# Modulations as rows on TensorE, the forget layer's head lengths inside its last projection block, and a delta layer without scaled keys and queries

## The chip, the cores and the metric

The kernel runs on one core of one Trainium2 chip. The metric is device time in microseconds of one execution; lower is better. All data is float32. A matmul that counts for accuracy is run as three matmuls in the type fp32r: both operands are split in a part `hi`, rounded to fp32r, and the rest `lo`, and hi·hi, lo·hi and hi·lo are added in PSUM (`triple`). Plain float32 matmuls appear in the trace as two instructions each.

## The reference

Eight layers run one after the other on x of 512 tokens by 1024. The first four are mixers (gated linear attention, spatial gating, forgetting attention, gated linear attention), each with its own modulation; the last four are dilated attention, a feed-forward layer, a gated delta layer and a feed-forward layer. What the change touches:

```
cond = silu(c)                                   # 1024 numbers
# layers 0 to 3: modulation i
mod = cond @ w_mod[i] + b_mod[i]                 # 3 x 1024: shift, scale, gate
h = rms_norm(x, norm_pre_g[i]) * (1.0 + scale) + shift
x = x + gate * rms_norm(mixer(h), norm_post_g[i])

# fox: 16 heads of 64
q, k, v, z, f_logit = split(h @ w_in)
q = rms_norm(q, g_q)                             # each head and token
k = rms_norm(k, g_k)
F = cumsum(log_sigmoid(f_logit + b_f))
o = softmax(causal(q @ k.T / 8 + F_i - F_j)) @ v
out = (o * silu(z)) @ w_out

# delta layer ("dn"): 6 heads of 128, memory of 256 tokens
qkv, z, gate_in, q_mem = split(h @ w_in)
q, k, v = split(silu(conv5(qkv)))                # 5 taps along the tokens
q = q * rsqrt(sum(q*q) + eps) * 128**-0.5
k = k * rsqrt(sum(k*k) + eps)
g = -exp(a_log) * softplus(gate_in + dt_bias);  beta = sigmoid(gate_in)
o = delta_rule(q, k, v, g, beta, chunks of 64)   # both directions, added
o = o * rsqrt(mean(o*o) + eps) * out_norm * silu(z)
mem = softmax(q_mem @ k_mem / 8) @ v_mem         # k_mem, v_mem from rms_norm(mem) @ w_kv
out = concat(o, mem) @ w_out
```

## The kernel before

The activations lie transposed in SBUF (`hT_hi`, `hT_lo`: 128 features by 8 tiles by 512 tokens). A projection is a list of blocks; a block has four chunks of 512 KB of weights (`w_raw`, six slots). For each chunk a DMA on SP's queue brings `w_raw`, ScalarE rounds it to `w_hi` (`act_feed`, L203), VectorE takes the rest to `w_lo` (`dve_feed`, L210), and TensorE runs its forms, most of them 128x512 outputs over two tiles of features, three matmuls each (L218 to L220). A block fills one of two sets of four PSUM banks, which ScalarE evacuates (`ps_evac`). Both feeds run ahead of TensorE by a few blocks, in an order written out by hand; every engine works in the order of its own program and waits on semaphores.

**Modulations.** For the first layer the 1024x2048 part of `w_mod` for shift and scale lies in four pieces in SBUF (`start_mod`, `hT_a`, `hT_b`), two tiles of rows (k) each. VectorE multiplies and adds k = 0 to 6 into `macc` (`dve_mod_first`, L490); TensorE then takes k = 7 (L500) and the sum of `macc` over the partitions (L504), both as matmuls with one column, 16 each, so that the result stands as columns. VectorE makes `modc` of it (L543, L544), and ScalarE applies it to the transposed, normed x (L752). L387 (`pe_bands`) makes tables that a later layer needs. For the layers after it the products are accumulated in `macc` by VectorE during the layer (`dve_mod`, L517, weights loaded by POOL's queue), and in the transition to the next layer `pe_mod` sums them over the partitions, again as 16 one-column matmuls (L532), and for the gate as two matmuls with 512 columns (L535). It is called `mid` there: it stands after the second chunk of the output projection, for token tiles 2 and 3; the same chunks' passes for tiles 0 and 1 come behind it and behind `g_ready`.

**The fox layer.** Blocks are projected in the order 4, 0, 1, 2, 3, 5, 6, 7 (v, q, k, v, z). After block 7, TensorE projects the 16 forget logits (`small_project`), ScalarE and VectorE make F (L1614 to L1616, L1657 to L1664), and then `norm_heads` runs for 16 tiles of 128 by 512 of q and k: ScalarE squares each (L1458), TensorE sums the squares over the heads into 32 rows of PSUM (L1445, `fox_sums`), ScalarE takes the root (L1460), VectorE the reciprocal (L1465) and its two parts (L1466, L1467), TensorE spreads a tile's rows to 128 partitions with two matmuls (L1451, L1452), and VectorE multiplies (L1470). Then the attention units begin (L1558 logits, L1560 decay, L1694 row maxima on VectorE).

**The dn layer.** Blocks 5, 0 to 4, 6 (z; q, k, v; q_mem), each of the middle ones followed by the convolution on VectorE (L2668, five taps, four tiles) and the silu on ScalarE (L2502). After block 6: 24 gate rows by `small_project`, turned (L2435), gate arithmetic (L2515 to L2519), the norm of the memory and its 16 transposes (L569 to L592, L601), the block `kv`, cumulated gates (L2446, L2447), the memory attention (L1744, L1751, L1760), and then `norm_heads` for 12 tiles with 12 rows (L1445). Only then do the six heads start: `decay_pe` (L2346), products, the inverse of a triangular matrix in doubling steps (L2323 to L2336), and the walk through the chunks with which the heads before are finished.

## Time and profile before

| | us |
|---|---|
| median of 3 runs | 2821.45 (2817.26 to 2822.45) |
| the profiled execution, device time | 2830.14 |
| its span | 2828.4 |
| TensorE busy / VectorE / ScalarE / GpSimd, of the span | 91% / 50% / 38% / 10% |

The profiled execution took 8.7 us longer than the median. The span runs from the first to the last instruction that the profiler saw. TensorE is busy in most of the 40 slices of the page; its granted clock is at full speed in most of them and at half in stretches in which it did little before. The chain that ended last tells, at each time, which engine the end waits for.

### The profile page before, as it was taken

Reading aid. Unit: us, or ns where it says so; the run is one execution under the profiler, and the core shown is the slowest. Engines: PE = TensorE matmul, PEld = TensorE weight load, DVE = VectorE, ACT = ScalarE, POOL = GpSimd, SP = SyncE. Lnnn points to the kernel's source line nnn. Section 1 sums busy time; section 2 is a strip of 40 time slices with the busy share of each in tenths; the row PEclk is TensorE's granted clock in tenths of the full one; section 3 lists DMA queues with packets and bytes.
Section 4 is the critical chain, followed back from the end, with each engine's and each line's share of the span. In section 5 each row is a group of like instructions: output and inputs, shape, how many; then the busy total and the mean of one; then the engine's idle time right before and its main releaser. Section 6 shows DMA issues by size and latency. Waiting matters only on the chain.

```text
span 2828.4 us, 32984 instructions
## 1 busy us (share of the span) xinstructions
PE 2582.8 (91%) x13022; PEld 2091.2 (74%) x13022; DVE 1410.2 (50%) x2386; ACT 1068.7 (38%) x1931; POOL 269.1 (10%) x420
## 2 busy tenths in 40 slices
PE   6989899999898989999878999999977998999998
PEld 4667778778446767787647888888854888888887
DVE  4666576555275656562244433325844666434322
ACT  4355342332443545453433322224244553322212
POOL 5233011011000013100000000001001110000000
PEclk7989999999989999999978999999977999999999
DMA  5522365256101412132101333324220000233332
GB/s 215 184 70 68 104 217 171 91 171 187 67 31 45 141 48 60 54 122 60 45 30 60 97 97 97 97 84 119 83 75 1 1 1 1 75 104 97 97 97 75
DMA packets 146228, 250.16 MB, mean 88 GB/s; under 512 B 15455, under 2 KB 65914, under 8 KB 145049
## 3 DMA queue, kind: packets, MB, share of 16 engines
q1 hardware_dynamic: 129008, 198.08, 22.4%
q0 software_dynamic: 14816, 48.31, 5.1%
q8 instruction: 104, 1.70, 0.2%
q10 hardware_dynamic: 2249, 1.65, 0.2%
q14 instruction: 51, 0.42, 0.1%
HBM read 245.84 MB, written 5.30 MB: 89 GB/s over the span
## 4 chain that ended last, share of the span: by engine, by line
PE 76%; DVE 9%; ACT 8%; DMA 3%; issue 2%; POOL 0%; SPq 0%; DVEq 0%; ACTq 0%
PE PS L218 20%; PE PS L219 19%; PE PS L220 19%; PE PS L985 2%; ACT tmp L752 1%; DMA hT_b<-in_w_mod 1%; PE PS L1760 1%; PE PS L1445 1%; DVE x L808 1%; PE PS L2323 1%; PE PS L2331 1%; PE PS L2336 1%; PE PS L1744 1%; PE PS L1581 1%; ACT w_hi L203 1%
## 5 line engine op out<-in xcount | busy, mean ns | idle before, releaser
L210 DVE TENSOR_TENSOR w_lo<-w_raw,w_hi 128x1024 fp32r<-128x1024 f32 (+1 forms) x344 | 412.7, 1207 | 782.3 <-ACT w_hi L203 781.3
L203 ACT ACTIVATE w_hi<-w_raw 128x1024 fp32r<-128x1024 f32 (+1 forms) x344 | 356.5, 1045 | 1041.9 <-DMA w_raw<-in_ffn_w_gate_up 310.1
L218 PE MATMUL PS<-hT_hi,w_hi 128*128 128x512 f32 (+1 forms) x1728 | 662.2, 383 | 21.7 <-DVE hT_lo L820 13.8
L219 PE MATMUL PS<-hT_lo,w_hi 128*128 128x512 f32 (+1 forms) x1728 | 653.3, 378 | 0.0
L220 PE MATMUL PS<-hT_hi,w_lo 128*128 128x512 f32 (+1 forms) x1728 | 653.1, 378 | 0.0
L218 PEld LDWEIGHTS PS<-hT_hi,w_hi 128*128 128x128 f32 x1728 | 331.2, 192 | 85.2 <-issue 19.0
L220 PEld LDWEIGHTS PS<-hT_hi,w_lo 128*128 128x128 f32 x1728 | 331.2, 192 | 59.9
L219 PEld LDWEIGHTS PS<-hT_lo,w_hi 128*128 128x128 f32 x1728 | 331.9, 192 | 56.6 <-issue 0.2
L218 PE MATMUL PS<-w_hi,hT_hi 128*128 128x512 f32 (+1 forms) x704 | 290.2, 412 | 32.0 <-DVE w_lo L210 7.7
L219 PE MATMUL PS<-w_lo,hT_hi 128*128 128x512 f32 (+1 forms) x704 | 278.8, 396 | 0.0
L220 PE MATMUL PS<-w_hi,hT_lo 128*128 128x512 f32 (+1 forms) x704 | 278.8, 396 | 0.0
L218 PEld LDWEIGHTS PS<-w_hi,hT_hi 128*128 128x128 f32 x704 | 141.2, 201 | 67.3 <-issue 15.1
L219 PEld LDWEIGHTS PS<-w_lo,hT_hi 128*128 128x128 f32 x704 | 141.5, 201 | 27.0 <-issue 1.8
L220 PEld LDWEIGHTS PS<-w_hi,hT_lo 128*128 128x128 f32 x704 | 140.2, 199 | 27.9
L517 DVE SCALAR_TENSOR_TENSOR macc<-mraw,cond,macc 128x512 f32<-128x512 f32 x160 | 122.1, 763 | 36.6 <-DMA mraw<-in_w_mod 33.8
L218 PE MATMUL PS<-w_hi,ffn_hi 128*128 128x512 f32 x352 | 139.4, 396 | 0.0
L220 PE MATMUL PS<-w_hi,ffn_lo 128*128 128x512 f32 x352 | 139.2, 395 | 0.0
L219 PE MATMUL PS<-w_lo,ffn_hi 128*128 128x512 f32 x352 | 139.2, 395 | 0.0
L462 POOL DMA_DIRECT2D mraw<-in_w_mod x160 | 86.3, 540 | 423.3 <-DVE macc L517 420.4
L985 PE MATMUL PS<-gla_E 128*128 128x128 f32 x448 | 62.5, 284 | 22.2 <-DVE gla_E L1204 22.1
L985 PEld LDWEIGHTS PS<-gla_E 128*128 128x128 f32 x448 | 58.2, 196 | 32.7 <-issue 30.3
L220 PEld LDWEIGHTS PS<-w_hi,ffn_lo 128*128 128x128 f32 x352 | 66.2, 188 | 16.0
(563 smaller groups left out, 3419.9 us busy)
## 6 DMA issues: line engine op xcount, KB each, us to landing
w_raw<-in_ffn_w_gate_up SPq DMA_DIRECT2D x176, 256.0 KB, 3.1
mraw<-in_w_mod POOLq DMA_DIRECT2D x160, 256.0 KB, 4.0
w_raw<-in_gla_w_in SPq DMA_DIRECT2D x48, 512.0 KB, 4.6
w_raw<-in_ffn_w_down SPq DMA_DIRECT2D x44, 512.0 KB, 3.8
w_raw<-in_fox_w_in SPq DMA_DIRECT2D x32, 512.0 KB, 4.1
w_raw<-in_sgu_w_in SPq DMA_DIRECT2D x24, 512.0 KB, 4.8
w_raw<-in_dn_w_in SPq DMA_DIRECT2D x24, 512.0 KB, 3.5
w_raw<-in_gla_w_out SPq DMA_DIRECT2D x16, 512.0 KB, 4.6
```

Of the source, the lines that this page charges most:

```text
L203: nc.scalar.activation(w_hi[:, n % NS, :, 0:m], w_raw[:, n % NS, :, 0:m], ACT.Copy).then_inc(w_hidone, 1)
L210: nc.vector.tensor_tensor(w_lo[:, n % NS, :, 0:m], w_raw[:, n % NS, :, 0:m], w_hi[:, n % NS, :, 0:m].bitcast(F32), ALU.subtract).then_inc( ...
L218: nc.tensor.matmul(o, l_hi, r_hi, start=start, stop=False)
L219: nc.tensor.matmul(o, l_hi, r_lo, start=False, stop=False)
L220: return nc.tensor.matmul(o, l_lo, r_hi, start=False, stop=stop)
L462: eng.dma_start(mraw[:, n % MS, 0, :], w[:, i % KT, m * BW:(m + 1) * BW]).then_inc(p_landed[n % MS], 16)
L517: nc.vector.scalar_tensor_tensor(out=acc, in0=mraw[:, n % MS, 0, :], scalar=cond[:, i % KT:i % KT + 1], in1=acc, op0=ALU.mult, op1=ALU.add ...
L752: ins = a.activation(tmp[:, k * P:(k + 1) * P], PS[:, 2 * t + k // 4, (k % 4) * P:(k % 4 + 1) * P], ACT.Identity, scale=nxt.scale[:, k:k + 1],
L808: v.tensor_tensor(x[:, t, :], x[:, t, :], y, ALU.add).then_inc(x_done, 1)
L985: mm = pe_.matmul(PS[:, l % 2, ts], a, m, start=True, stop=True)
L1445: t_.matmul(PS[0:nr, bank, :], sums[:, nr - per * n:2 * nr - per * n], sq(n), start=n == 0, stop=n == n_tiles - 1).then_inc(lens.sum, 1)
L1581: mm = t_.matmul(PS[rows, 5 + (h // 2) % 2, t * P:(t + 1) * P], r.v[:, k, h * FD:(h + 1) * FD], PT[:, u2 % 2, k * P:(k + 1) * P], start=k ...
```

## The change

Three parts in one kernel.

**Modulations as rows.** For the first layer, TensorE does all of it: the bias by four matmuls with one row, and for each k four matmuls with 32 columns (of `cond`, repeated 32 times) and 512 elements, which write to four groups of 32 partitions of one bank (L485, L492 in the new numbering). `dve_mod_first` and the memset ahead of it are gone; the band tables are made between k = 3 and 4. VectorE copies the bank to SBUF, TensorE turns it by four transposes (`pe_mod_turn`, L499), and VectorE makes `modc` of the columns. For layers 1 to 3 the 16 one-column matmuls become four with 32 columns, and copy, turn and `modc` follow in the same way; TensorE waits for `modc_done` ahead of the passes for tiles 0 and 1.

**Fox.** The squares of tiles 0 to 7 are made on ScalarE after the evacuation of block 5, those of 8 to 15 after that of block 6. The sums go to four column groups of one bank (tile n to rows 32·(n mod 4)), tiles 0 to 7 and the forget logits between the first and the second chunk of the last block, tiles 8 to 15 behind the second. Root, reciprocal and the two parts are made on 128 rows. The spreads of tiles 0 to 3 (`lengths`) stand between the forms of the last chunk, the other twelve behind it; the multiplication is as before. VectorE feeds the last four chunks of weights ahead of the attention behind its 16 multiplications, where it did so ahead of F before.

**Dn.** The norm of the memory moves into the first two blocks. The 12 squares are made on ScalarE behind the silu of block 2, the gate rows and the 12 sums stand ahead of block 6, the turns of the gates in the middle of it, and the turns of the lengths in the middle of `kv`. q and k are not scaled: beta is divided by |k|²+eps, the values are scaled by the root of |k|²+eps on their way out of PSUM (four ScalarE instructions in place of one), and the length of q goes into the epsilon of the output's norm (one more VectorE instruction of 128x4 a head). `norm_heads` is removed.

```diff
-        M0 = KT - 1
-
-        def dve_mod_first():
-
-            v = nc.vector
-            v.wait_ge(m_row, mod_rows(0))
-            v.wait_ge(cond_done, 1)
-            for k in range(M0):
-                if k % 2 == 0:
-                    v.wait_ge(m0_landed[k // 2], 16)
-                v.scalar_tensor_tensor(out=macc[:, 0:4 * BW], in0=first_mod[k // 2][:, k % 2, :], scalar=cond[:, k:k + 1],
-                                       in1=macc[:, 0:4 * BW], op0=ALU.mult, op1=ALU.add).then_inc(m0_used, 1)
-                v.wait_ge(m0_used, k + 1)
-
         def pe_mod_first(bank):
 
             t_ = nc.tensor
             t_.wait_ge(cond_done, 1)
-            t_.wait_ge(m0_landed[M0 // 2], 16)
-            for j in range(2 * KT):
-                t_.matmul(PS[:, bank, 2 * j:2 * j + 1], first_mod[M0 // 2][:, M0 % 2, j * P:(j + 1) * P], cond[:, M0:M0 + 1],
-                          start=j == 0, stop=False)
-            t_.wait_ge(m0_used, M0)
-            for j in range(2 * KT):
-                mm = t_.matmul(PS[:, bank, 2 * j:2 * j + 1], macc[:, j * P:(j + 1) * P], ones[:, 0:1],
-                               start=False, stop=j == 2 * KT - 1)
+            t_.wait_ge(m_row, mod_rows(0))
+            for j in range(4):
+                t_.matmul(PS[32 * j:32 * j + 32, bank, :], ones[0:1, 0:32], macc[0:1, j * BW:(j + 1) * BW], start=True, stop=False)
+            for k in range(KT):
+                if k % 2 == 0:
+                    t_.wait_ge(m0_landed[k // 2], 16)
+                if k == KT // 2:
+                    pe_bands()
+                for j in range(4):
+                    mm = t_.matmul(PS[32 * j:32 * j + 32, bank, :], cond[:, k:k + 1].to_broadcast([P, 32]),
+                                   first_mod[k // 2][:, k % 2, j * BW:(j + 1) * BW], start=False, stop=k == KT - 1)
             mm.then_inc(mfin, 1)
+
+        def pe_mod_turn(s, bank):
+            nc.tensor.wait_ge(mrows, s + 1)
+            for m in range(4):
+                mm = nc.tensor.transpose(PS[:, bank, m * P:(m + 1) * P], hf[:, 0, m * P:(m + 1) * P], ident[:])
+            mm.then_inc(mturned, 1)
...
-                for j in range(2 * KT):
-                    mm = nc.tensor.matmul(PS[:, banks[0], 2 * j:2 * j + 1], macc[:, j * P:(j + 1) * P], ones[:, 0:1],
+                for j in range(4):
+                    mm = nc.tensor.matmul(PS[32 * j:32 * j + 32, banks[0], :], ones[:, 0:32], macc[:, j * BW:(j + 1) * BW],
...
+                nc.vector.tensor_copy(hf[:, 0, :], PS[:, banks[0], :]).then_inc(mrows, 1)
...
+                nc.vector.wait_ge(mturned, s + 1)
+                nc.vector.tensor_copy(by4(modc[:, s % 2, 1, :]), v[:, 0:2])
+                nc.vector.scalar_tensor_tensor(out=by4(modc[:, s % 2, 0, :]), in0=v[:, 2:4], scalar=1.0,
+                                               in1=by4(vcol("pre", KT * s)), op0=ALU.add, op1=ALU.mult).then_inc(modc_done, 1)
...
+                            if L < DEPTH:
+                                pe_mod_turn(L, cur.mod_bank)
+                                t_.wait_ge(modc_done, L + 1)
                             t_.wait_ge(*cur.g_ready)
...
+                z = wb[-1]
+
+                def chunk(c, after=lambda j: None):
+                    t_.wait_ge(w_lodone, z.first + c + 1)
+                    for j, form in enumerate(T_forms(z)):
+                        for k in range(CK):
+                            mm = form_pass(form, z.first + c, c, k, hT_hi, hT_lo, c == 0 and k == 0, c == z.n - 1 and k == CK - 1)
+                        if j == 3:
+                            mm.then_inc(w_used, 1)
+                        after(j)
+
+                def sums(n0, n1):
+                    for n in range(n0, n1):
+                        g, m = 32 * (n % 4), n // 4
+                        t_.wait_ge(lens.sq, n + 1)
+                        t_.matmul(PS[g:g + 32, 0, :], r.sums[:, 2 * FH - 2 * m:4 * FH - 2 * m], sq[n % NSQ],
+                                  start=m == 0, stop=m == 3).then_inc(lens.sum, 1)
+
+                def lengths(n):
+                    g, m = 32 * (n % 4), n // 4
+                    if n >= 2:
+                        t_.wait_ge(lens.nrm, n - 1)
+                    for s in range(2):
+                        mm = t_.matmul(PS[:, 2 + n % 2, :], ajunk_r[g:g + 32, m * P:(m + 1) * P], tmp_r[g:g + 32, s, :],
+                                       start=s == 0, stop=s == 1)
+                    mm.then_inc(lens.sum, 1)
+
+                t_.wait_ge(ps_evac, z.before.ev)
+                chunk(0)
+                t_.wait_ge(ps_evac, wb[-2].ev)
+                t_.wait_ge(q.bones, 1)
+                sums(0, NP)
                 small_project(1, FH)
-                t_.wait_ge(q.bones, 1)
-                nh.pe()
+                chunk(1)
+                sums(NP, 2 * NP)
+                chunk(2)
+                t_.wait_ge(lens.rows, 1)
+                chunk(3, lengths)
+                for n in range(4, 2 * NP):
+                    lengths(n)
+                t_.wait_ge(ps_evac, z.ev)
...
+                    if n == 7:
+                        squares(NSQ, 2 * NP)
+                        a.wait_ge(small.mm, 2)
+                        a.wait_ge(q.cols, 80)
+                        z, bf = r.FR[0:FH, 0, :], r.gains[0:FH, 2:3]
+                        then_act(a.activation(z, PS[0:FH, 1, :], ACT.Abs, bias=bf))
+                        then_act(a.activation(z, z, ACT.Exp, scale=-1.0))
+                        a.activation(z, z, ACT.Ln, bias=1.0).then_inc(q.lz, 1)
+                        a.wait_ge(lens.sum, 2 * NP)
+                        a.activation(root, PS[:, 0, :], ACT.Sqrt, bias=eps[:]).then_inc(lens.root, 1)
...
+                    if n == 5:
+                        a.wait_ge(ps_evac, b.before.ev + 1)
+                        a.wait_ge(m_used, NMC * (i + 1))
+                        squares(0, NSQ)
...
-                nh.dve()
+                v.wait_ge(lens.root, 1)
+                then_dve(v.reciprocal(root, root))
+                then_dve(v.tensor_copy(tmp_r[:, 0, :], root))
+                v.tensor_tensor(tmp_r[:, 1, :], root, tmp_r[:, 0, :].bitcast(F32), ALU.subtract).then_inc(lens.rows, 1)
+                for n in range(2 * NP):
+                    v.wait_ge(lens.sum, 2 * NP + n + 1)
+                    v.scalar_tensor_tensor(out=tile(n), in0=tile(n), scalar=r.gains[:, n % 2:n % 2 + 1], in1=PS[:, 2 + n % 2, :],
+                                           op0=ALU.mult, op1=ALU.mult).then_inc(lens.nrm, 1)
+                dve_feed(ahead(wb[-1]))
...
+                part(wb[1], T_forms(wb[1]), 0, 2)
+                pre_pe(mq, [(ps_evac, wb[0].ev)], 2, halves_of)
+                part(wb[1], T_forms(wb[1]), 2, 4)
+                t_.wait_ge(mem_x.hf, 2 * KT)
+                for b in wb[2:6]:
+                    pe_block(b, T_forms(b), hT_hi, hT_lo)
+                t_.wait_ge(ps_evac, wb[4].ev)
+                small_project(3, 24, 2)
+                t_.wait_ge(q.mask, 1)
+                t_.wait_ge(lens.sq, L0 + 2 * NH)
+                for n in range(2 * NH):
+                    z, m = 32 * (n % 4), n // 4
+                    t_.matmul(PS[z:z + 32, 3, :], r.sums[:, 32 - m:64 - m], sq[n], start=m == 0, stop=m == 2).then_inc(lens.sum, 1)
+                last = [("T", bank_set(wb[6]) + j, j * P) for j in range(2)]
...
+                part(kv, kv_forms, 0, 2, m_.hi, m_.lo)
+                t_.wait_ge(lens.rows, 2)
+                t_.wait_ge(small.read, 2)
+                for c in range(TT):
+                    mm = t_.transpose(PS[:, 2, cs(c)], sq[0][:, cs(c)], ident[:])
+                mm.then_inc(lens.root, 1)
+                part(kv, kv_forms, 2, 4, m_.hi, m_.lo)
...
-                nh.pe()
...
+                        a.wait_ge(ps_evac, b.ev)
+                        a.wait_ge(mem_x.split, 2 * KT)
+                        for m in range(2 * NH):
+                            a.activation(sq[m], tile(m), ACT.Square).then_inc(lens.sq, 1)
...
-                    a.activation(d_.v[:, n % 2, :], PS[:, 5, :], ACT.Copy).then_inc(q.vte, 1)
+                    for c in range(TT):
+                        ins = a.activation(d_.v[:, n % 2, cs(c)], PS[:, 5, cs(c)], ACT.Identity, scale=r.ss[:, c, n:n + 1])
...
+                v.wait_ge(lens.root, 2)
+                lengths = PS[:, 2, :].rearrange("p (c a z w) -> p c a z w", c=TT, a=2, z=2)[:, :, :, :, 0:NH // 2]
+                pairs = lambda a: a.rearrange("p c (m a) -> p c a m", a=2)
+                v.tensor_scalar(pairs(r.bq[:]), lengths[:, :, :, 0, :], EPS, EPS * P, ALU.add, ALU.mult)
+                then_dve(v.tensor_scalar(pairs(r.ss[:]), lengths[:, :, :, 1, :], EPS, None, ALU.add))
+                then_dve(v.reciprocal(r.rk[:], r.ss[:]))
+                for d in range(2):
+                    ins = v.tensor_tensor(r.beta[:, :, NH * d:NH * d + NH], r.beta[:, :, NH * d:NH * d + NH], r.rk[:], ALU.mult)
+                then_dve(ins)
+                v.tensor_scalar(r.nbeta[:], r.beta[:], -1.0, None, ALU.mult).then_inc(q.gdve, 1)
...
+                        v.scalar_tensor_tensor(out=d_.rt[:], in0=PS[:, 6, 0:TT], scalar=1.0 / P, in1=r.bq[:, :, k],
+                                               op0=ALU.mult, op1=ALU.add).then_inc(q.root, 1)
```

TensorE's order at the start, behind the transposes of the first token tiles; `start_mod`, `hT_a` and `hT_b` hold the modulation's weights. Before:

```order
L632 MATMUL PS<-ident,gla0x_xn 128x128 x16
L500 MATMUL PS<-cond,hT_b 128x1 x16
L504 MATMUL PS<-ones,macc 128x1 x16
L387 MATMUL PS<-start_tabs,start_table 4x512 x3
L218 MATMUL PS<-w_hi,hT_hi 128x512
```

After:

```order
L630 MATMUL PS<-ident,gla0x_xn 128x128 x16
L485 MATMUL PS<-macc,ones 32x512 x4
L492 MATMUL PS<-start_mod,cond 32x512 x16
L387 MATMUL PS<-start_tabs,start_table 4x512 x3
L492 MATMUL PS<-hT_a,cond 32x512 x8
L492 MATMUL PS<-hT_b,cond 32x512 x8
L499 MATMUL PS<-ident,tmp 128x128 x4
L220 MATMUL PS<-w_hi,hT_hi 128x512
```

The 32 one-column matmuls are gone, and the tables stand ahead of the last 16 of the matmuls that take their place.

TensorE's order from the end of the fox layer's last block to the first logits; `small_hi` are the weights of the forget logits. Before:

```order
L220 MATMUL PS<-hT_hi,w_lo 128x512
L218 MATMUL PS<-hT_hi,small_hi 16x512
...
L220 MATMUL PS<-hT_hi,small_lo 16x512
L1445 MATMUL PS<-mraw,fox_sums 32x512 x16
L1451 MATMUL PS<-hT_hi 128x512
L1452 MATMUL PS<-hT_lo,hT_hi 128x512
...
L1558 MATMUL PS<-fox_kT,fox_qT 128x128 x2
```

After, from the end of the first chunk of that block:

```order
L222 MATMUL PS<-hT_hi,w_lo 128x512
L1552 MATMUL PS<-fox_szT,fox_sums 32x512 x4
L1552 MATMUL PS<-mraw,fox_sums 32x512 x4
L220 MATMUL PS<-hT_hi,small_hi 16x512
...
L1552 MATMUL PS<-fox_szT,fox_sums 32x512 x4
L1552 MATMUL PS<-mraw,fox_sums 32x512 x4
...
L1560 MATMUL PS<-tmp_r,ajunk_r 128x512 x2
L220 MATMUL PS<-hT_hi,w_hi 128x512
...
L1560 MATMUL PS<-tmp_r,ajunk_r 128x512 x26
L1594 MATMUL PS<-fox_kT,fox_qT 128x128 x2
```

The sums and the logits' projection moved into the block, and 26 of the 32 spreading matmuls stand behind it.

TensorE's order in the dn layer from the gate rows to the first decays. Before:

```order
L220 MATMUL PS<-hT_hi,small_lo 24x512
L2435 MATMUL PS<-ident,dn_P 128x24 x4
L601 MATMUL PS<-ident,dn_xn 128x128 x16
...
L1760 MATMUL PS<-dn_PT,dn_mv 64x128 x4
L1445 MATMUL PS<-dn_AT,dn_sums 12x512 x12
L1451 MATMUL PS<-hT_hi,identr 128x512
L1452 MATMUL PS<-hT_lo,identr 128x512
...
L2346 MATMUL PS<-dn_tri,dn_g 128x128 x8
```

After:

```order
L222 MATMUL PS<-hT_hi,small_lo 24x512
L2506 MATMUL PS<-dn_squares,dn_sums 32x512 x4
...
L2511 MATMUL PS<-ident,ajunk 128x24 x4
...
L2521 MATMUL PS<-ident,dn_squares 128x128 x4
...
L1816 MATMUL PS<-dn_PT,dn_mv 64x128 x4
L2401 MATMUL PS<-dn_tri,dn_g 128x128 x8
```

The memory's transposes left this stretch for block 0, the sums stand ahead of block 6 instead of behind the memory attention, and between the memory attention and the decays nothing is left.

## Rows read from the trace of the kernel before

**Rows 1.** The page: chain by engine; its costliest group: busy us, mean ns, idle.

```profile
PE 76%; DVE 9%; ACT 8%; DMA 3%; issue 2%; POOL 0%; SPq 0%; DVEq 0%; ACTq 0%
...
L210 DVE TENSOR_TENSOR w_lo<-w_raw,w_hi 128x1024 fp32r<-128x1024 f32 (+1 forms) x344 | 412.7, 1207 | 782.3 <-ACT w_hi L203 781.3
```

**Rows 2.** Busy us (count) of PE, PEld, DVE, ACT, POOL by stretch; then clock.

```profile
299.51:307.20 7.69, 7.69 (x37) 5.62 (x37) 1.84 (x2) 0.00 (x0) 0.00 (x0) 0.67 0.00 0
509.84:516.30 6.46, 6.46 (x36) 4.68 (x37) 0.00 (x0) 0.00 (x0) 0.00 (x0) 0.81 0.00 0
600.00:700.00 100.00, 100.00 (x443) 82.81 (x442) 51.71 (x57) 29.49 (x24) 20.58 (x42) 1.00 0.64 202
773.31:790.72 17.41, 16.48 (x33) 8.14 (x33) 11.96 (x16) 0.00 (x0) 0.00 (x0) 0.50 0.00 1
896.75:904.35 7.60, 7.60 (x37) 5.53 (x37) 0.00 (x0) 0.00 (x0) 0.00 (x0) 0.68 0.00 0
```

**Rows 3.** The chain of waits at the start: start us, us, what.

```profile
2.95 28.18 DMA hT_b<-in_w_mod
31.27 6.96 PE PS L500 x32
38.23 6.84 PE PS L504 x32
45.49 2.91 ACT tmp L752 x8
...
50.53 0.77 PE PS L218
```

**Rows 4.** The timeline at the start: ScalarE's first rounding of weights.

```profile
32.88 1.06 ACT L203 ACTIVATE w_hi<-w_raw 128x1024 fp32r<-128x1024 f32 x1 [14.12 <-DMA w_raw<-in_gla_w_in]
```

**Rows 5.** The chain in a transition without one-column matmuls.

```profile
1182.14 1.72 PE PS L535 x4
```

**Rows 6.** The chain: matmuls into 64-column halves, and into all columns.

```profile
803.63 0.88 PE PS L1581 x12
...
2222.75 0.89 PE PS L2323 x8
```

**Rows 7.** The fox layer: the chain, one line's matmuls, and VectorE's timeline.

```profile
738.11 1.89 ACT fox_szT L1608
...
751.18 14.90 PE PS L1445 x28
...
768.75 3.35 DVE mraw L1465
...
L1445 PE MATMUL PS<-mraw,fox_sums x32: 592/592/1057, 751.2 to 767.2; 128*32 128x512 f32 x32
...
L1470 DVE SCALAR_TENSOR_TENSOR fox_qT<-fox_qT,fox_gains,PS x8: 746/748/749, 774.6 to 789.0; 128x512 f32<-128x512 f32 x8
...
791.77 0.29 DVE L1694 CUSTOM_DVE_ANT_0 mraw<-PS,fox_FR 128x128 f32<-128x128 f32 x1 [1.20 <-PE PS L1560]
```

**Rows 8.** Busy time by stretch in the dn layer, columns as in Rows 2.

```profile
2058.30:2069.10 10.80, 10.80 (x50) 8.91 (x48) 7.75 (x12) 3.26 (x4) 0.00 (x0) 1.00 0.55 178
2069.10:2098.25 29.15, 11.72 (x46) 6.42 (x44) 12.53 (x32) 16.13 (x28) 0.00 (x0) 0.70 0.07 25
2098.25:2117.10 18.85, 15.81 (x102) 15.54 (x102) 5.63 (x7) 6.33 (x7) 0.00 (x0) 0.77 0.35 112
2117.10:2141.74 24.64, 22.26 (x130) 12.78 (x129) 14.66 (x69) 15.69 (x55) 0.74 (x2) 0.84 0.00 1
2141.74:2171.57 29.83, 24.33 (x49) 7.81 (x49) 12.00 (x14) 8.63 (x13) 1.59 (x3) 0.73 0.00 0
```

**Rows 9.** ScalarE in the dn layer: one instruction of its timeline, and one line's.

```profile
2029.60 1.92 ACT L2502 ACTIVATE dn_qkvT<-dn_qkvT 128x2048 f32<-128x2048 f32 x1 [14.50 <-DVE dn_qkvT L2668]
...
L1458 ACT ACTIVATE dn_AT<-dn_qkvT x12: 612/629/630, 2141.0 to 2152.3; 128x512 f32<-128x512 f32 x12
```

**Rows 10.** VectorE's small reciprocal in the six heads.

```profile
L2788 DVE RECIPROCAL dn_rt<-dn_rt x6: 172/178/179, 2250.0 to 2396.1; 128x4 f32<-128x4 f32 x6
```

More of the change, by code:

```diff
@@ L2427, in pe, with part @@
                 t_ = nc.tensor
-                for n, b in list(zip(kinds, wb))[1:]:
-                    forms = T_forms(b) if n < 6 else [("T", bank_set(b) + j, j * P) for j in range(2)]
-                    pe_block(b, forms, hT_hi, hT_lo)
-                t_.wait_ge(ps_evac, wb[-1].ev)
-                small_project(3, 24)
+                def part(b, forms, c0, c1, a_hi=hT_hi, a_lo=hT_lo):
+                    if c0 == 0 and b.before:
+                        t_.wait_ge(ps_evac, b.before.ev)
+                    for c in range(c0, c1):
+                        t_.wait_ge(w_lodone, b.first + c + 1)
+                        for form in forms:
+                            for k in range(CK):
+                                mm = form_pass(form, b.first + c, c, k, a_hi, a_lo, c == 0 and k == 0, c == b.n - 1 and k == CK - 1)
+                        mm.then_inc(w_used, 1)
@@ L2433, in pe @@
+                last = [("T", bank_set(wb[6]) + j, j * P) for j in range(2)]
+                part(wb[6], last, 0, 2)
                 t_.wait_ge(small.read, 1)
                 for t in range(TT):
[L2435 removed]
+                    mm = t_.transpose(PS[:, 2, 32 * t:32 * t + 24], gateT[:, t * P:(t + 1) * P], ident[0:24, 0:24])
                 mm.then_inc(small.turned, 1)
[L2437 removed]
+                part(wb[6], last, 2, 4)
@@ L2495, in act @@
                 for n, b in zip(kinds, wb):
+                    if n == 6:
+                        a.wait_ge(lens.sum, 2 * L0 + 2 * NH)
+                        a.activation(sq[0], PS[:, 3, :], ACT.Copy).then_inc(lens.rows, 1)
                     act_feed(ahead(b))
@@ L2650, in dve @@
                 for n, b in zip(kinds, wb):
+                    if n == 6:
+                        v.wait_ge(small.mm, 4)
+                        v.tensor_copy(gateT, PS[0:24, 2, :]).then_inc(small.read, 1)
                     dve_feed(ahead(b))
+                    if n == 5:
+                        pre_dve_rows(mq, mem_raw, 2)
+                        dve_feed(ahead(wb[1]) - 2)
+                        pre_dve_cols(mq, m_.hi, m_.lo, 2)
                     if n >= 5:
@@ L2834, in dve @@
                         if h and lv == 6:
-                            gate_dve(k, 1)
-                for part in (2, 3):
+                            gate_dve(k, 2)
+                for part in (3, 4):
                     gate_dve(NH - 1, part)
```

142 lines of the change are left out of this document (64 added, 78 removed).

## Prediction

> **What bounds the kernel now.** I read the page's chain first: 76% of it is TensorE, 9% VectorE, 8% ScalarE, 3% DMA [rows 1]. The kernel is bound by TensorE's own stream, at full clock 0.226 us a matmul (443 in 100 us) [rows 2], and by the places where that stream stops or runs slowly. VectorE's costliest group is the weights' low parts, 1.21 us each, 344 of them [rows 1]; it waits most of its time, so work can be put there where it has a gap. The views by stretch then give the places that the diff touches. At the start TensorE's first projecting matmul comes at 50.53, behind a DMA that lands at 31.13 and 14 us of one-column matmuls [rows 3]. Three transitions hold 7.69, 6.46 and 7.60 us of modulation matmuls, at a mean clock of 0.67 to 0.81 [rows 2]; one without the one-column matmuls takes 1.72 for the same gate matmuls [rows 5]. In the fox layer block 7 ends at 738, the first row maximum on VectorE comes at 791.77 [rows 7]: 53.8 us. In the dn layer the stretch from 2058.30 to 2171.57, the first decays, is 113.3 us in five pieces at a clock of 0.70 to 1.00 [rows 8]. All sums are made against the profiled execution (2830.14, of which the span is 2828.4); it took 8.7 more than the median of the runs, 2821.45, and the difference is taken off at the end.
>
> **One price comes into all parts:** a float32 matmul with 32 columns and 512 elements, four of which write to four column groups. One alone is two instructions; those of the fox layer take 0.592 each as recorded, and their line's stretch of 14.90 us keeps pace with ScalarE's squares, not with itself [rows 7]. Full-width matmuls of 512 go at 0.226 in fp32r; float32 takes two instructions at twice that, so 0.85 a matmul, 3.4 for four one after another. For column groups side by side the trace has only halves: 12 matmuls in 64-column halves take 0.88, 8 in all columns 0.89 [rows 6]. If halves overlap nearly fully, quarters should. Between 0.86 and 3.4 I take 1.1 for a group of four, since rows 6 are the nearest.
>
> The Trainium skill ("TensorE: Matmul & The Clock Gate", Part 3, Measured speedup) gives 2.38 times for three column tiles with M = 32, N = 512; an estimate from that page and 0.85 is 1.1 for three and little more for four. By an estimate of 1.2 for four the twelve groups that count below would cost 1.2 more in all, 2729 instead of 2728; no run here shows it.
>
> **Start.** Removed: L500 and L504, 13.9 us behind the DMA [rows 3]. Added: the groups for k = 0 to 5 and the tables run while the DMA is under way; behind 31.13 stand those of the last piece, two groups, 2.2. So the sum ends at 33.5 instead of 45.1. Then a copy of 128x512 out of PSUM (0.7; a multiplication of that size out of PSUM takes 0.748 [rows 7]), four transposes (0.6), two small operations (0.3): 35.4, where ScalarE's L752 starts at 45.49 now. All behind it moves: the rounding of weights was done at 32.88 already [rows 4], so the first chunk is there. Gain **10.0**. If the clock is still at half there, the two groups and the transposes cost 2.5 more. The first layer then asks for weights 10 us earlier.
>
> **Transitions.** From 7.69, 6.46, 7.60 [rows 2] and about 0.8 of matmuls at half clock behind the first and third, to one group (1.1), the gate matmuls as in rows 5 (1.7) and, at the end of the early passes, a turn and a wait (1.4). VectorE's copy of 0.7 stands ahead of its gate products, under TensorE's passes; its wait for `mturned` holds back the splits of weights queued behind it, and the turn stands behind at most two chunks' passes, of which the weights are there. 4.3, 2.7 and 4.2: **11.2**.
>
> **Fox.** Block 7's 96 matmuls take 21.8 and end ahead of 738.1 [rows 7], so it starts at 716.1. From there TensorE now has: the 96 matmuls (21.8), the logits' projection (24 at 0.227, 5.5), four groups of sums (4.4), a wait for reciprocal and parts (3.35 for 32 rows now [rows 7], and the same for 128 since its length is 512 a row; it lies under the third chunk but for 0.5), eight spreading matmuls (1.8). About 20 changes between column groups, row groups and full width lie in it; around L1581 I saw gaps of some 0.1, and take 1.0 in all, between 0 and 2. The block ends at 751.1. Behind it twelve tiles go at VectorE's pace: 0.748 a multiplication [rows 7] and 0.05, 9.6. The spreads, which run at half clock now (17.41 us, clock 0.50 [rows 2], so that VectorE waits for them), need only be faster than that. Then VectorE feeds four chunks, 1.21 each [rows 1], ahead of the first maximum: 4.8. So 765.7 instead of 791.8: **26.1**. If the feed were hidden it would be 31.
>
> The Trainium skill ("TensorEngine Tiling (Array Packing)", Key Properties) says that changing the tiling mode drains TensorE. It gives no price. By that rule each of the 20 changes would cost what I saw, 0.1, so 2.0 instead of 1.0, and the time would be 2729; the trace shows such gaps around L1581 alone.
>
> **Dn.** The twelve squares, 0.63 each [rows 9], go behind block 2's silu. ScalarE waited 14.5 us for the convolution just ahead of such a silu [rows 9], so most of the 7.6 fits, but a silu that comes later holds the next convolution: I take 1.6, between 0 and 7.6. Then the stretch from 2058.30: gate rows 5.5, sums 3.3 (three groups), block 6 10.8 as now [rows 8], turns 0.5. The piece of 29.15 us with the gates' arithmetic and the memory's norm [rows 8] goes but for that: the norm is done in the first blocks, and the arithmetic runs beside `kv`. The piece with `kv`, 18.85 at clock 0.77 [rows 8], no longer follows a pause: TensorE's 15.81 would be 12.2 at full clock, of which I count 2.9 as gained: 15.95. Turns of the lengths 0.5. The memory attention stays, 24.6 less a square of 0.7 at its end [rows 8]: 23.9; it depends on gate factors that now have a longer chain of small operations and one more load of tables: 1.3. The last piece, 29.83 [rows 8], goes but for 0.5. Together 64.0 (with 1.6 for the stall) against 113.3, less 1.8 for the 16 transposes that block 0 now carries: **47.5**.
>
> **Heads.** One more VectorE operation of 128x4 a head, 0.18 [rows 10], six of them, in a piece in which VectorE is the one waited for: **+1.2**. Four ScalarE instructions instead of one for the values lie beside other work; POOL loses waits.
>
> Sum: 10.0 + 11.2 + 26.1 + 47.5 − 1.2 = 93.6. 2830.1 − 93.6 = 2736.5 in a profiled execution, and 2821.45 − 93.6 = **2728** for the median.
>
> **Rivals.**
> (a) *The column groups run one after another.* For it: L1445, all in one group, shows nothing of overlap. Against: rows 6. Each group then costs 3.4 instead of 1.1. The start has nine groups and the tables (5.3) to run, from where `cond` is made, some 12 us ahead of the landing: 18.9 + 30.8 + 5.3 = 55.0 instead of 33.5, 22 later; transitions 7, fox 9, dn 7. 45 in all: 2773.
> (b) *The work put into the blocks stalls them.* Squares, roots and the logits' chain stand on ScalarE ahead of the rounding of weights, which VectorE's splits and TensorE wait for. Against it: both engines are ahead of TensorE by a block or so, some 20 us; for it: twelve squares in dn and eight twice in fox are 5 to 8 us at once. It gives back about 15: 2743.
> (c) *The start's gain is given back* since the first layer waits for its weights and the modulation's loads, which share the DMA engines with it: 10 back: 2738.
> (d) *Slower than before.* The groups run one after another and, as few columns are at work, TensorE's clock falls to half around them, as around the one-column matmuls (0.67 [rows 2]). A group is then 6.8: start 52 late, transitions 23, fox 53 (its block 7 at half clock), dn 41: 169 back, 2897. It decides beyond 93.6 back, which needs more than 5 us a group over what I took, with the neighbours slowed. Against it: L1445's matmuls with 32 columns at a median of 0.592 [rows 7], the length of full clock; its maximum, 1.057, is the length at half.
> (e) *Better than forecast:* feed and squares hidden, the memory attention (clock 0.84 [rows 8]) at full clock: 15 to 20 more, 2710.
>
> **How the numbers follow.** Forecast 0.62, (a) 0.08, (b) 0.12, (c) 0.08, (d) 0.01, (e) 0.09. The unknown costs: groups 0.86 or 3.4, stall 0 to 7.6, changes 0 to 2, feed 0 or 4.8, kv's gain 0 to 3.6; profile against median some 4. Low end: 4.8 + 1.6 + 1.0 + 3.9 (memory attention) + 2.9 (12 groups at 0.86) + 0.7, with heads at 0 and 4 for the run, about 20, and some 8 for what becomes earlier elsewhere: 2700. High end: (b) and (c) together, 2753, with the stall at its end and part of (a): 2770. What a measurement can tell from no change is 0.2%, 5.6 us; all cases but (d) and a wait that I don't see lie far on one side: faster 0.97, same 0.01, slower 0.02.
>
> **What the changed kernel's profile would show.** Modulation matmuls of the first layer beside the DMA, `modc` at about 35, the first projecting matmul at about 40.5. In the transitions a group of four in about 1.1 and no fall of the clock. Block 7 of fox about 35 us long with no wait over 1, first maximum some 50 us after its start. In dn no stretch of over 5 us without matmuls between block 6 and the decays, and 64 us from the end of block 5 to them. The forecast is wrong if four matmuls in four groups take 3.4 us, if TensorE waits for `w_lo` in the blocks that took in squares, or if the first layer waits at 60 to 85 us for weights or modulation loads that now come no sooner.

## The result and the profile after

| | median us | range | runs |
|---|---|---|---|
| before | 2821.95 | 2817.26 to 2826.32 | 4 |
| changed | 2729.94 | 2725.81 to 2740.73 | 4 |

The ratio is 0.968 (95% interval 0.9647 to 0.9713), 92.0 us less, where 93.6 less (2728) was forecast. The profiled execution took 2727.18 with a span of 2725.2. That of before took 2830.14, 8 above its median, so the two traces stand 103 apart, 11 more than the times: a term that is read from these two traces alone can come out too large by some of that.

The page of the changed kernel, the lines that answer to [rows 1]:

```profile
PE 77%; DVE 9%; ACT 8%; DMA 4%; issue 3%; POOL 0%; SPq 0%; DVEq 0%; ACTq 0%
...
L212 DVE TENSOR_TENSOR w_lo<-w_raw,w_hi 128x1024 fp32r<-128x1024 f32 (+1 forms) x344 | 411.8, 1206 | 744.1 <-ACT w_hi L205 743.1
```

Nothing else has become the bound. VectorE's idle time ahead of its splits (the low parts of the weights) fell by 38 us. That TensorE's stream has fewer holes, so that its feeders wait less, is my reading of it.

The chain of waits at the start, to be read against [rows 3] (L387 makes the tables, L492 the modulation's rows, L537 copies them, L499 turns them):

```profile
2.36 23.59 DMA hT_a<-in_w_mod
25.99 2.76 PE PS L387 x6
28.75 5.24 PE PS L492 x32
34.01 0.70 DVE tmp L537
34.76 0.67 PE PS L499 x4
35.78 2.91 ACT tmp L753 x8
...
40.81 0.77 PE PS L220
```

ScalarE applies the modulation at 35.78 instead of 45.49, and the first projecting matmul comes at 40.81 instead of 50.53. Behind the landing of `hT_a` stand the tables, the rows of the last two pieces of weights, and 0.7 + 0.7 of copying and turning.

The chain in the first and the third transition, where [rows 2] had 7.69 and 7.60:

```profile
288.00 1.00 PE PS L526 x8
289.00 1.91 PE PS L529 x4
...
851.10 0.99 PE PS L526 x8
852.10 1.92 PE PS L529 x4
```

The fox layer: the chain through block 7, then VectorE's timeline from the first multiplication to the first row maximum (L1723 is the multiplication, L1560 the spreading, L1552 the sums):

```profile
702.27 1.85 PE PS L1552 x16
...
715.25 1.85 PE PS L1552 x16
...
724.35 0.66 PE PS L1560 x2
725.01 0.43 PE PS L220
...
725.04 0.75 DVE L1723 SCALAR_TENSOR_TENSOR fox_qT<-fox_qT,fox_gains,PS 128x512 f32<-128x512 f32 x1 [2.41 <-PE PS L1560]
727.30 0.75 DVE L1723 SCALAR_TENSOR_TENSOR fox_kT<-fox_kT,fox_gains,PS 128x512 f32<-128x512 f32 x1 [1.51 <-PE PS L1560]
...
743.15 0.75 DVE L1723 SCALAR_TENSOR_TENSOR fox_kT<-fox_kT,fox_gains,PS 128x512 f32<-128x512 f32 x1 [0.41 <-PE PS L1560]
743.82 4.62 DVE L212 TENSOR_TENSOR w_lo<-w_raw,w_hi 128x1024 fp32r<-128x1024 f32 x4
748.36 0.28 DVE L1750 CUSTOM_DVE_ANT_0 mraw<-PS,fox_FR 128x128 f32<-128x128 f32 x1
```

Busy time by stretch in the dn layer and its first head (columns as in Rows 2), to be read against [rows 8]; the stretches are gate rows, sums and block 6; `kv`; the memory attention up to the first decays; the first head up to the next head's decays:

```profile
2011.40:2031.20 19.80, 19.80 (x101) 12.31 (x100) 12.97 (x17) 6.66 (x8) 0.00 (x0) 1.00 0.34 101
2031.20:2043.00 11.80, 11.80 (x101) 11.80 (x99) 4.96 (x11) 9.74 (x13) 0.00 (x0) 1.00 0.53 178
2043.00:2072.22 29.22, 24.20 (x137) 14.35 (x135) 17.75 (x77) 19.72 (x59) 0.00 (x0) 0.82 0.08 24
2072.22:2091.23 19.01, 12.60 (x68) 11.74 (x69) 10.60 (x25) 7.46 (x21) 8.30 (x10) 0.73 0.00 0
```

60.8 us from the end of block 5 to the decays instead of 113.3. In the first two TensorE is busy all the time at full clock.

To place the rest I matched the projecting matmuls of two traces one by one (both kernels have 8640 in the same order but for the moved pieces) and read the difference of their times at stations. Length of each stretch in us, from traces of seven kernels; the three of the changed kernel show what executions differ by. "Gaps + banks" and "best" come below. Stretches that are not listed are left out, so the columns don't add up to the span.

| stretch | before | changed, 3 traces | rows only | no fox | no dn | gaps + banks | best |
|---|---|---|---|---|---|---|---|
| to the first projecting matmul | 50.5 | 40.8, 40.0, 40.3 | 40.7 | 40.1 | 42.3 | 44.3 | 40.1 |
| from there to transition 1 | 248.6 | 246.8, 245.6, 247.1 | 246.9 | 243.5 | 246.9 | 247.6 | 246.7 |
| fox, end of block 7's first chunk to the output projection | 168.2 | 143.5, 143.5, 143.9 | 168.1 | 168.1 | 143.7 | 137.5 | 136.8 |
| third transition and the fourth layer | 279.5 | 277.3, 276.5, 273.7 | 274.0 | 276.3 | 274.2 | 273.1 | 276.7 |
| dn, end of block 5 to the first decays | 112.9 | 60.8, 60.7, 60.8 | 109.8 | 61.8 | 108.1 | 60.7 | 58.6 |
| of it, end of `kv` to the first decays | 59.1 | 29.2, 29.1, 29.2 | 57.8 | 30.2 | 56.6 | 29.1 | 27.0 |
| dn's heads, first decays to the output projection | 231.1 | 227.0, 227.1, 227.1 | 231.3 | 229.7 | 233.6 | 226.9 | 229.7 |
| output projection and the last layer | 418.0 | 418.1, 418.2, 418.0 | 417.7 | 417.8 | 417.8 | 418.1 | 417.5 |

Two of the rows say how far a single trace can be trusted. The dn layer of "rows only" and of "no dn" is that of before, and from block 5's end to the decays it takes 109.8 and 108.1 there: the trace of before (112.9; it is 113.3 in [rows 8], counted from 0.3 earlier) was 3 to 5 slower in this stretch than these. And the first projecting matmul comes between 40.0 and 44.3 in kernels whose start is the same, though `hT_a` lands at 25.7 to 26.1 in all of them. Most of the difference is TensorE's clock behind that landing: at 1.00 from 26 to 35 us in the second and third trace of the changed kernel (40.0 and 40.3), at 0.50 to 0.52 in "gaps + banks" (44.3), where the tables take 5.18 instead of 2.76.

### The profile page after: what moved, and what is told of

Its sections match the earlier page's. It is cut to its first block, busy times and chain, and to the rows that moved or that the text cites. A ratio compares the mean times of both kernels' runs of the same rounds, so it can differ in the third digit from the quotient of the medians.

```text
span 2725.2 us, 32853 instructions
## 1 busy us (share of the span) xinstructions
PE 2518.7 (92%) x12954; PEld 2047.7 (75%) x12954; DVE 1381.8 (51%) x2380; ACT 1068.8 (39%) x1951; POOL 254.0 (9%) x420
## 4 chain that ended last, share of the span: by engine, by line
PE 77%; DVE 9%; ACT 8%; DMA 4%; issue 3%; POOL 0%; SPq 0%; DVEq 0%; ACTq 0%
PE PS L220 21%; PE PS L221 20%; PE PS L222 20%; PE PS L985 2%; ACT tmp L753 2%; PE PS L1816 1%; PE PS L2378 1%; DVE x L809 1%; DMA hT_a<-in_w_mod 1%; PE PS L2386 1%; PE PS L2391 1%; PE PS L1800 1%; ACT w_hi L205 1%; PE PS L1617 1%; DMA mraw<-in_w_mod 1%
## 5 line engine op out<-in xcount | busy, mean ns | idle before, releaser
L220 PE MATMUL PS<-hT_hi,w_hi 128*128 128x512 f32 (+1 forms) x1728 | 663.2, 384 | 21.5 <-DVE hT_lo L821 13.9
L220 PEld LDWEIGHTS PS<-hT_hi,w_hi 128*128 128x128 f32 x1728 | 331.2, 192 | 88.4 <-issue 22.6
L220 PE MATMUL PS<-w_hi,hT_hi 128*128 128x512 f32 (+1 forms) x704 | 288.0, 409 | 37.2 <-DVE hT_lo L821 10.4
L220 PEld LDWEIGHTS PS<-w_hi,hT_hi 128*128 128x128 f32 x704 | 140.2, 199 | 70.3 <-issue 17.7
L220 PE MATMUL PS<-w_hi,ffn_hi 128*128 128x512 f32 x352 | 139.5, 396 | 0.0
L985 PE MATMUL PS<-gla_E 128*128 128x128 f32 x448 | 62.9, 285 | 21.2 <-DVE gla_E L1204 21.1
## 6 DMA issues: line engine op xcount, KB each, us to landing
w_raw<-in_ffn_w_gate_up SPq DMA_DIRECT2D x176, 256.0 KB, 3.1
mraw<-in_w_mod POOLq DMA_DIRECT2D x160, 256.0 KB, 4.1
```

Of the source, the lines that this page charges most:

```text
L220: nc.tensor.matmul(o, l_hi, r_hi, start=start, stop=False)
L985: mm = pe_.matmul(PS[:, l % 2, ts], a, m, start=True, stop=True)
```

## The experiments

Kernels that are compared ran beside the kernel before on one chip: the first four in one set (before: 2825.63), the next four in a second (2827.33), the last four in a third (2827.59).

### Each part by itself

`p_rows` is the kernel before with the modulations as rows alone:

> The kernel before with the modulations as rows alone (all four layers); fox and dn as before. By my terms 10.0 + 11.2 less than before, and some 2 more that the changed kernel's first layer shows behind the start: 23 less, about 2799. Rival: the parts are not additive, and what the modulations give is given back at the next wait (the first layer's loads): 10 to 15 less, 2807 to 2812.

`no_fox` and `no_dn` are the changed kernel with one of the other parts undone (all of its hunks taken back):

> The changed kernel with the fox part undone. By the trace of the changed kernel the fox layer gives 25.4: 2755. By the rival that the profiled execution of before was slow there for another reason, less than 20: under 2750.

> The changed kernel with the dn part undone. By the forecast dn with its heads gives 46.3: 2776. By the two traces it gives 54, of which 3 are at the first head, which finds TensorE's clock and ScalarE's table as it needs them: 2784.

| | median us | ratio to before (95%) | what it isolates |
|---|---|---|---|
| rows only | 2804.89 | 0.9922 (0.9905 to 0.9939) | rows: 20.7 (forecast 21.2) |
| no fox | 2755.12 | 0.9744 (0.9727 to 0.9761) | fox, against 2729.94: 25.2 (26.1) |
| no dn | 2776.64 | 0.9824 (0.9807 to 0.9841) | dn and heads, against 2729.94: 46.7 (46.3) |

The three add up to 92.6, where the whole change gives 92.0. The rival of `p_rows` (10 to 15 only) is out, though its 20.7 is 2 short of what my reading of the traces, 23, said. The 2729.94 comes from another set, whose kernel before took 3.7 less. By the changed kernel's three ratios to before (0.968 here, 0.9659 and 0.9669 below) it would have taken 2729.3 to 2735.2 beside these runs, which makes fox 19.9 to 25.8 and dn with its heads 41.4 to 47.3. So that both differences lie within 1 of their terms is closer than these runs can tell, and the sum is known to lie between 82 and 94 only: that the parts don't disturb each other is shown to about 10. The 54 that the two traces give for dn and its heads is outside in any case. Part of it is the slow stretch in the trace of before.

### The groups of 32 columns

```diff
-                    mm = t_.matmul(PS[32 * j:32 * j + 32, bank, :], cond[:, k:k + 1].to_broadcast([P, 32]),
+                    mm = t_.matmul(PS[0:32, bank, :], cond[:, k:k + 1].to_broadcast([P, 32]),
```

> The changed kernel, but in the first layer the four matmuls of a k all write to the first group of 32 columns, so they can't run side by side; shift and scale of that layer come out wrong. If the four groups side by side are what makes the rows cheap, a k takes 3.4 instead of 0.86 at full clock, the 32 matmuls no longer fit in before the last landing, and the first projecting matmul comes 15 to 22 later: about 2750. If column groups don't matter (the rows wait for their DMA anyway), no more than 3 later.

Measured: 2747.71 (2744.60 to 2753.25), ratio 0.9716 (0.9696 to 0.9735). The chain at its start:

```profile
20.47 13.85 PE PS L492 x32
34.32 2.67 PE PS L387 x6
36.99 13.87 PE PS L492 x32
...
50.88 0.70 DVE tmp L537
```

and one line of the timeline of the changed kernel, the same 32 instructions (16 matmuls) in four groups:

```profile
19.87 3.64 PE L492 MATMUL PS<-start_mod,cond 128*32 128x512 f32 x32
```

13.85 in one group against 3.64 in four: 3.8 times faster. In one group an instruction starts every 0.43 us; in four groups four start together every 0.43. Both run at full clock (each is recorded with 0.592 in either). So a group of four matmuls (two instructions each) is 0.9 us, not the 1.1 that I took, and the copy comes 16.9 later (50.88 against 34.01), as does the first projecting matmul (57.68 against 40.81), within my 15 to 22. Of rival (a) this is the price at the start; of (d), the fall of the clock around few columns, nothing is seen even in 28 us of such matmuls.

### The fox layer's multiplications and the weights behind them

Two edits of the changed kernel, alone and together. `fox_gaps`:

```diff
                 for n in range(2 * NP):
+                    if n < 4:
+                        dve_feed(ahead(wb[-1]) - 3 + n)
                     v.wait_ge(lens.sum, 2 * NP + n + 1)
...
-                dve_feed(ahead(wb[-1]))
```

> The changed kernel, but the four low parts of weights that VectorE made behind its 16 multiplications in the fox layer are made one each ahead of the first four, where it waits 1.5 to 2.4 us for TensorE. If they stand on the path, 4.6 less. If the attention behind them is bound by something else (ScalarE's table, the logits), 0 to 1 less.

`fox_banks`:

```diff
-                    if n >= 2:
-                        t_.wait_ge(lens.nrm, n - 1)
+                    if n >= 3:
+                        t_.wait_ge(lens.nrm, n - 2)
...
-                        mm = t_.matmul(PS[:, 2 + n % 2, :], ajunk_r[g:g + 32, m * P:(m + 1) * P], tmp_r[g:g + 32, s, :],
+                        mm = t_.matmul(PS[:, (2, 3, 1)[n % 3], :], ajunk_r[g:g + 32, m * P:(m + 1) * P], tmp_r[g:g + 32, s, :],
```

> The changed kernel with three PSUM banks for the spread lengths instead of two. If the pace of 1.03 a multiplication (0.80 was forecast) is the handing over of a bank from VectorE to TensorE and back, the twelve behind the block fall to 0.80 each: 2.7 less. If TensorE's own spreading sets the pace, nothing.

VectorE's timeline in `fox_banks`:

```profile
733.17 0.75 DVE L1723 SCALAR_TENSOR_TENSOR fox_kT<-fox_kT,fox_gains,PS 128x512 f32<-128x512 f32 x1 [1.50 <-PE PS L1560]
733.84 0.74 DVE L1723 SCALAR_TENSOR_TENSOR fox_qT<-fox_qT,fox_gains,PS 128x512 f32<-128x512 f32 x1
734.50 0.74 DVE L1723 SCALAR_TENSOR_TENSOR fox_kT<-fox_kT,fox_gains,PS 128x512 f32<-128x512 f32 x1
...
741.24 0.75 DVE L1723 SCALAR_TENSOR_TENSOR fox_kT<-fox_kT,fox_gains,PS 128x512 f32<-128x512 f32 x1
```

From the fourth to the sixteenth multiplication it is 8.07 us, 0.67 each, with no wait; with two banks 11.36 (731.79 to 743.15), 0.95 each, with waits of 0.16 and 0.41 for L1560. So the pace that I had mis-sized was the handing over of the bank, and a multiplication itself goes at 0.67, less than the 0.75 that its record shows: the records of successive ones overlap. The same timeline in `fox_gaps` (L1725 is the multiplication there):

```profile
728.79 0.75 DVE L1725 SCALAR_TENSOR_TENSOR fox_qT<-fox_qT,fox_gains,PS 128x512 f32<-128x512 f32 x1 [1.27 <-PE PS L1560]
729.46 1.22 DVE L212 TENSOR_TENSOR w_lo<-w_raw,w_hi 128x1024 fp32r<-128x1024 f32 x1
731.04 0.75 DVE L1725 SCALAR_TENSOR_TENSOR fox_kT<-fox_kT,fox_gains,PS 128x512 f32<-128x512 f32 x1 [0.36 <-PE PS L1560]
...
748.34 0.29 DVE L1751 CUSTOM_DVE_ANT_0 mraw<-PS,fox_FR 128x128 f32<-128x128 f32 x1 [1.20 <-PE PS L1596]
```

The splits fit into the waits, and the first maximum waits 1.2 for TensorE's first logits, which the feed had covered. The stretch from block 7's end to the output projection is 114.7 in the changed kernel, 111.8 with the gaps (2.9 less where 4.6 was expected; that wait is 1.2 of the 1.7 that are missing) and 111.2 with the banks (3.5 less; 2.7 expected). The times, 2730.93 (ratio 0.966, 0.9629 to 0.9691) and 2727.95 (0.9661, 0.9633 to 0.9689), can't tell either from the changed kernel beside them, 2729.11 (0.9659, 0.9640 to 0.9679).

> The changed kernel itself, on the chip and beside the runs of the three that follow. On the chip of the part-by-part runs its parts add up to 2727; so 2725 to 2732. A second profile: if the difference of the first two profiles in the dn layer's heads (4 less) was the clock of that execution and not the change, the heads differ between the two profiles of this kernel by as much.

> The changed kernel with both edits of the fox layer: the four low parts ahead of the first four multiplications, and three banks for the spread lengths. Alone they shorten the stretch from the end of block 7 to the output projection from 114.7 to 111.8 and 111.2. If they are independent (VectorE's chain is the path in both), 108.3; if both only uncover TensorE's and ScalarE's start of the attention, 111.

`after_again` gave the 2729.11 above, and its heads in the dn layer take 227.1 where the first trace had 227.0. So the 4 less against before were no chance of one execution, though other kernels with the same dn code have 229.7 (below).

Measured for `fox_both`: 108.7 for the stretch, 6.0 less, where 2.9 and 3.5 are 6.4, so the two are nearly independent; 2725.07 us, ratio 0.9643 (0.9618 to 0.9669), an interval that still overlaps the changed kernel's.

### The last chunk of weights at kv

`kv_late` rounds that chunk behind the memory attention:

```diff
-                act_feed(ahead(kv))
+                act_feed(ahead(kv) - 1)
                 a.wait_ge(w_used, kv.last + 1)
...
                 mem.act(lambda w, src: (r.oT[:, w.local_pair, :], src))
+                act_feed(ahead(kv))
```

and the same with `dve_feed` on VectorE.

> The changed kernel, but the last chunk of weights that is rounded ahead of the evacuation of kv in the dn layer (its DMA lands 2 us after TensorE has stopped) is rounded behind the memory attention. If ScalarE's wait for that DMA is what TensorE waits for there, 3 less; if the gates' chain on VectorE is as late, 0 to 1 less.

Measured: 2727.20, ratio 0.9649 (0.9632 to 0.9667). ScalarE's timeline: the evacuation now waits 0.87 for TensorE itself and starts at `kv`'s end, where it started 2.0 behind it before the edit; the two table loads follow:

```profile
2045.69 0.60 ACT L2614 ACTIVATE dn_mk<-PS 128x512 f32<-128x512 f32 x1 [0.87 <-PE PS L222]
2046.18 0.59 ACT L2615 ACTIVATE dn_mv<-PS 128x512 f32<-128x512 f32 x1
2046.79 1.28 ACT L2617 ACT_TABLE_LOAD   x1
...
2048.31 1.28 ACT L2619 ACT_TABLE_LOAD   x1
```

But the chain has the rounding again, between the attention and the first head:

```profile
2072.93 1.06 ACT w_hi L205
```

From `kv`'s end to the decays it is 27.7 instead of 29.2, and the heads take 1.5 longer, all of it in the first one (20.6 instead of 19.0). There the second set of decays waits 2.9 for ScalarE's L2631 instead of 2.0, so 0.9 of the 1.5 is the moved work. The wait for the DMA was on the path; the place to which I moved the work was too.

`kv_slots` puts it behind the first head's decays on both engines, where the changed kernel's ScalarE waits 4.21 for L2418 and VectorE 3.72 for L2391, and makes the root ahead of the evacuation:

```diff
                 act_feed(ahead(kv) - 1)
+                a.wait_ge(q.gdve, 4)
+                a.activation(r.ss[:], r.ss[:], ACT.Sqrt)
                 a.wait_ge(w_used, kv.last + 1)
...
                 for d in range(2):
                     decay_act(0, d)
+                act_feed(ahead(kv))
```

> The changed kernel with the last chunk's rounding moved behind the first head's decays, where ScalarE waits 4.2 and VectorE 3.7 us, and with the root of |k|^2+eps made ahead of the evacuation of kv. If kv_late gained 2.0 at kv and gave it back at the first decays, the stretch from kv's end to the output projection falls from 256.3 by 2 to 3.5; if the gates were never on the path, nothing.

Measured: 2727.58, ratio 0.9654 (0.9635 to 0.9672). From `kv`'s end to the decays 27.2 instead of 29.2, but from there to the output projection 229.7 instead of 227.1, so 256.9 for both instead of 256.2. Against the changed kernel that is a miss. But kernels whose dn layer is the changed kernel's to the letter fall in two kinds: the changed kernel and `fox_both` with 256.0 to 256.3 for the whole stretch, and `fox_gaps`, `fox_banks` and `no_fox` with 259.9 to 260.0 (229.7 in the heads, as here). Against the second kind `kv_slots` gains 3, as expected, and TensorE's waits for ScalarE in its first head (2.0 ahead of L2401, 1.9 ahead of L2410) are as long as in `fox_gaps`, so the moved work isn't seen to cost anything. The 2 between `kv` and the decays are shown: 27.0 to 27.7 in the three kernels with the edit, 29.1 to 30.3 in all others with the new dn layer. What they are worth to the end is not.

### The edits together

> All of the two kernels before in one. Independent: 6 from fox and 3 from dn, 9 less than the changed kernel, 2720. If executions' own spread in the heads and in the first layer hides it, the stretches of the trace still show 6 and 3.

> The changed kernel once more beside these: 2729. If the best of the edits is real, its interval and this one's don't meet.

| | median us | range | ratio to before (95%) |
|---|---|---|---|
| best | 2722.99 | 2720.33 to 2726.51 | 0.9633 (0.9619 to 0.9646) |
| changed, beside it | 2730.95 | 2725.82 to 2744.11 | 0.9669 (0.9646 to 0.9693) |

8.0 less by the medians, 9 expected; the intervals meet at 0.9646 where I had said they wouldn't, so the gain isn't clear of the noise by that test. The traces show where it lies: fox 136.8 against 143.9, 7 less, and 2 less between `kv` and the decays. The heads take back 2.6 in this pair of traces, so the 2 at `kv` are not seen in the sum.

## Why the prediction was right, point by point

- **What bounds the kernel, and the form of the sum.** Right. A sum of 93.6 that was to leave TensorE's chain took 92.0 from the time, and the three parts by themselves came out within 1 of their terms, which is closer than runs of different sets can tell (up to 6 for fox and dn). Adding up the recorded steps gives slightly less than was written: the start 35.1 for 35.4, the second transition 2.3 for 2.7, fox 765.5 for 765.7, dn 63.85 for 64.0. Together they change the forecast by less than 1.
- **The price of a group of four.** 0.9 (3.64 for four groups, 0.99 for one in a transition) instead of 1.1; nearer to the end that rows 6 gave, 0.86. `one_group` shows 3.8 times for four. The estimate from the Trainium skill's three column tiles ("TensorE: Matmul & The Clock Gate", Part 3, Measured speedup), 1.2, was too high.
- **Start.** 10.0 forecast, 9.7 in the trace. The rows ended at 34.0, not 33.5: the tables run behind the landing of `hT_a`, for which TensorE stood idle 2.48, and the sixteen instructions on `hT_a` behind them ran at half clock (recorded with a median of 1.061 instead of 0.592). That it came out within 0.3 is in part luck: by the clock there, other traces of the same start have 6.2 to 10.5, and the forecast had put 2.5 on it. Rival (c) didn't come: the first layer, 248.6 before, is 245.6 to 247.1.
- **Transitions.** 4.3, 2.7 and 4.2 forecast. By the matched matmuls ahead and behind, 4.5, 3.0 and 4.6: 12.1 for 11.2. The clock stays full there, as foreseen. The turn takes 0.45 in the second transition, and TensorE then waits 0.3 for `modc`.
- **Fox.** 26.1 forecast, 24.7 by the traces, and 25.2 by times from two sets. Block 7 ended at 731.1, 34.4 after its start, for 35.1: the sums took 3.7 for 4.4, the reciprocal cost no wait for 0.5, and the changes of column and row groups 1.6 for 1.0. Going to 32-row groups costs some 0.2 on the way in (0.66 for two instead of 0.46) and 0.2 behind (0.43 for L220 instead of 0.23), and there are four such places. The rule of the Trainium skill ("TensorEngine Tiling (Array Packing)", Key Properties) that a change of mode drains TensorE agrees with these delays, for which it gives no price. Mis-sized was the term of the twelve multiplications: 9.6 forecast, 12.7 measured (731.1 to 743.8), because of the two banks. Feed: 4.6 for 4.8. `fox_gaps` shows that it was on the path, as said, for 2.9 of it; behind that the first logits are nearly as late.
- **Dn.** 64.0 with the stall forecast, 60.8 measured. The stall by the squares (1.6) didn't come: from block 0 to block 5's end the matched matmuls take 1.7 longer than before, and the 16 transposes alone are 1.75 (1.8 forecast). The stretch ahead of `kv` took 19.8 for 20.2. Cut at `kv`'s own end (the row of 18.85 ends 4.6 behind it), the forecast gives 11.9 for `kv` and 30.3 from there to the decays; measured were 11.8 and 29.2. In all it is 50.4 by the two traces, 47.5 forecast. But the old stretch varies by trace: against those of `p_rows` and `no_dn` (109.8 and 108.1) the gain is 47.3 and 45.6, on either side of the forecast.
- **Heads.** +1.2 forecast; the trace has −4.1, so here the sign was wrong. What I left out is the first head's start. Before, it came out of `norm_heads` with TensorE at half clock and ScalarE's table for the root:

```profile
2171.57:2193.73 22.16, 14.49 (x68) 13.46 (x69) 11.54 (x26) 8.35 (x19) 6.01 (x6) 0.59 0.00 1
...
2171.57 2.02 PE PS L2346 x8
...
2174.93 1.28 ACT L2539
```

  With `norm_heads` the table load is gone, and TensorE comes there at full clock (1.00 in the 12 us ahead of the decays, 0.50 before the change): the same 68 matmuls take 19.01 at a mean clock of 0.73 (above). That is 3.1 less; over all traces the first head takes 22.2 to 23.1 with the old dn layer and 19.0 to 20.6 with the new. The rest is within what heads differ by from trace to trace, so whether the extra operation costs its 1.2 is open.
- **The rivals.** (a) and (d) are refuted by `one_group` and the full clock. (b): in none of the blocks that took in work does TensorE wait. (e): the feed was not hidden. That the total came within 1.6 is partly luck: by the traces fox was put 1.4 too high and the transitions 0.9 and the heads 5.3 too low, and the executions themselves differ by that much.

## What to carry to other kernels

Float32 matmuls with 32 output columns are worth putting side by side in four groups; before such a step is moved into a block, ask whether its inputs are there. Where TensorE fills a PSUM bank and VectorE empties it in about the same time, two banks left a wait for the handing over at most steps here (0.95 a step), and a third took it away (0.67). A piece of work that is taken off the path at one place must be put where its engine waits, read from the trace; between two dependent stages it is on the path again.

## What the runs showed of the hardware

The time of a head in the dn layer comes in steps. The same head, with the same instructions, in the changed kernel and in `one_group` (whose dn layer is the same):

```profile
2153.66:2188.05 34.39, 30.98 (x268) 30.01 (x266) 24.73 (x65) 18.93 (x51) 5.07 (x6) 1.00 0.01 1
...
2167.81:2205.38 37.57, 34.17 (x267) 32.88 (x266) 24.74 (x65) 19.05 (x51) 5.08 (x6) 0.91 0.00 1
```

VectorE and ScalarE are busy alike; TensorE is busy 3.2 longer at a mean granted clock of 0.91 instead of 1.00. In `one_group` it is one fall: the clock is at 1.00 up to 2197.4, at 0.50 from 2197.8 to 2203.8, and rises again. Over all traces the middle heads take 32.9, 34.4, 36.0 or 37.6, steps of 1.6. The stretch of all heads was 226.9 to 227.1 in the three traces of the changed kernel and in `fox_both`, 228.6 in `kv_late`, 229.7 in five other variants and 240.7 in `one_group`. What sets these falls I can't say. They are as large as a small edit's gain, so an edit of some 3 us was judged here by its own stretch of the trace and not by the time.
